# Dense products of a hybrid decoder layer: the 544 tokens split at 512 in place of 272

## The reference

```python
x = x + 0.5 * swiglu_1(rmsnorm(x))                 # 1024 -> 2816 (gate, up) -> 1024
z = rmsnorm(x) @ w_in                              # 1024 -> 3608: mLSTM and GLA heads
x = x + concat(mlstm(z), gla(z)) @ w_out           # 1024 -> 1024
x = x + cross_attention(rmsnorm(x), memory)        # w_q, 256 memory tokens, w_o
x = x + 0.5 * swiglu_2(rmsnorm(x))
y = final_rmsnorm(x)
```

## Time and profile before

| | us |
|---|---|
| median of 2 runs (1354.36 to 1355.21) | 1354.78 |
| the profiled execution, its own time | 1352.57 |
| its span, first to last instruction | 1350.7 |
| TensorE busy (98%) | 1327.1 |
| weight loads busy (95%) | 1289.6 |
| DVE busy (49%) | 665.2 |
| ACT busy (32%) | 429.3 |
| mean granted TensorE clock, share of full | 0.995 |

### The profile page before, as it was taken

How to read it: one execution, slowest core, us unless ns; L and a number is a source line. 1 busy time by engine, 2 the same in 40 slices (tenths; PEclk the granted TensorE clock), 3 DMA queues, 4 the chain that set the end, 5 groups by cost and what they waited for, 6 DMA issues and landing times.

```text
span 1350.7 us, 25765 instructions
## 1 busy us (share of the span) xinstructions
PE 1327.1 (98%) x11027; PEld 1289.6 (95%) x11027; DVE 665.2 (49%) x903; ACT 429.3 (32%) x644; POOL 41.8 (3%) x64
## 2 busy tenths in 40 slices
PE   8999999999999999999999999999999999999997
PEld 8999999999999999998888898889999999999997
DVE  5445455443333377667676534535545445443332
ACT  6222222222222243345434612323322222222222
POOL 1000000000000000002111000100000000000000
PEclk9999999999999999999999999999999999999998
DMA  6332323323333333224145664533232232323221
GB/s 198 95 92 79 93 82 88 89 73 88 91 79 95 81 79 80 79 79 126 35 124 191 220 208 141 212 101 94 79 93 86 85 93 81 90 85 88 86 71 67
DMA packets 208136, 138.31 MB, mean 102 GB/s; under 512 B 6550, under 2 KB 196224, under 8 KB 208068
## 3 DMA queue, kind: packets, MB, share of 16 engines
q1 hardware_dynamic: 200240, 109.88, 28.1%
q0 software_dynamic: 7664, 27.27, 6.1%
q10 hardware_dynamic: 164, 0.16, 0.0%
HBM read 129.41 MB, written 7.88 MB: 102 GB/s over the span
## 4 chain that ended last, share of the span: by engine, by line
PE 48%; DVE 1%; ACT 1%; issue 0%; another core or an unknown queue 0%; ACTq 0%
PE ps L1690 47%; PE ps L2135 1%; PE ps L2239 0%; ACT prob L873 0%; PE ps L2164 0%; DVE xmx L1563 0%; PE ps L2085 0%; DVE kT L1580 0%; PE ps L2113 0%; ACT kT L884 0%; DVE v_own L1457 0%; DVE y_raw L1401 0%; DVE prob L1572 0%; ACT y_hi L805 0%
## 5 line engine op out<-in xcount | busy, mean ns | idle before, releaser
L1690 PE MATMUL ps<-xn_hi,w_hi 128*128 128x272 f32 x2144 | 447.2, 289 | 0.9 <-ACT xn_hi L573 0.9
L1690 PE MATMUL ps<-xn_hi,w_lo 128*128 128x272 f32 x2144 | 444.1, 288 | 0.0
L1690 PE MATMUL ps<-xn_lo,w_hi 128*128 128x272 f32 x2144 | 442.7, 287 | 0.6 <-DVE xn_lo L985 0.6
L551 ACT ACTIVATE w_hi<-raw 128x1024 fp32r<-128x1024 f32 x206 | 218.0, 1058 | 642.5 <-PE ps L1690 642.5
L967 DVE TENSOR_TENSOR w_lo<-raw,w_hi 128x1024 fp32r<-128x1024 f32 x206 | 252.3, 1225 | 201.8 <-ACT w_hi L551 200.7
L1690 PEld LDWEIGHTS ps<-xn_hi,w_hi 128*128 128x128 f32 x2144 | 336.1, 188 | 2.1 <-DVE w_lo L967 1.1
L1690 PEld LDWEIGHTS ps<-xn_hi,w_lo 128*128 128x128 f32 x2144 | 337.7, 189 | 0.0
L1690 PEld LDWEIGHTS ps<-xn_lo,w_hi 128*128 128x128 f32 x2144 | 336.1, 188 | 1.0 <-DVE xn_lo L985 0.8
L1690 PE MATMUL ps<-h_hi,w_hi 128*128 128x272 f32 x704 | 145.9, 289 | 0.0
L1690 PE MATMUL ps<-h_hi,w_lo 128*128 128x272 f32 x704 | 145.3, 288 | 0.0
L1690 PE MATMUL ps<-h_lo,w_hi 128*128 128x272 f32 x704 | 144.9, 287 | 0.0
(11 more groups left out here) (345 smaller groups left out, 1087.4 us busy)
## 6 DMA issues: line engine op xcount, KB each, us to landing
raw<-in_ffn_w_gate SPq DMA_DIRECT2D x44, 512.0 KB, 3.9
raw<-in_ffn_w_up SPq DMA_DIRECT2D x44, 512.0 KB, 3.8
raw<-in_w_in SPq DMA_DIRECT2D x29, 512.0 KB, 3.8
raw<-in_ffn_w_down SPq DMA_DIRECT2D x32, 448.0 KB, 3.7
raw<-in_ffn_w_down SPq DMA_DIRECT2D x16, 512.0 KB, 3.9
kv<-in_cache_mem_k POOLq DMA_DIRECT2D x6, 1024.0 KB, 6.3
kv<-in_cache_mem_v POOLq DMA_DIRECT2D x6, 1024.0 KB, 6.9
raw<-in_w_out SPq DMA_DIRECT2D x8, 512.0 KB, 4.1
```

What stands on the lines that cost most here:

```text
L551: act.activation(w_hi[u0 % 2][:, :], raw[u0 % 4][:, :], ACT.Copy).then_inc(sem("hi_done"), 1)
L1690: return pe.matmul(out, lhsT, rhs, start=start, stop=stop)
```

## The change

A pair of halves becomes a long part of 512 tokens (the prompt, TP) and a short part of 32 (the sample). The long part fills the first bank of its pair, the short part columns 0 to 31 of the second, so that the 544 results lie in one run and `halves` becomes the identity. The waits by half follow the new parts: the first needs all four prompt chunks, the second the sample too. The small decay product, in its own banks, keeps 272 and 272.

```diff
@@ pair @@
-            return ps[:, q:q + 2, 0:HT]
+            return ps[:, q:q + 2, :].rearrange("p b c -> p (b c)")[:, 0:T]
+
+        SPLIT = [(0, TP), (TP, T)]
@@ halves @@
-            return t2d.rearrange("p (h t) -> p h t", h=2)
+            return t2d
@@ norm @@
-                mm(pair(buf)[:, 0, :], ones, acc[:, 0:HT])
-                mm(pair(buf)[:, 1, :], ones, acc[:, HT:T]).then_inc(sem("norm_mm"), 1)
+                mm(pair(buf)[:, 0:TP], ones, acc[:, 0:TP])
+                mm(pair(buf)[:, TP:T], ones, acc[:, TP:T]).then_inc(sem("norm_mm"), 1)
@@ unit @@
-                            ins = mm(ps[:, 2 * (buf % 4) + half, 0:HT], w, m[:, k0 + j, half * HT:(half + 1) * HT],
+                            t0, t1 = SPLIT[half]
+                            ins = mm(ps[:, 2 * (buf % 4) + half, 0:t1 - t0], w, m[:, k0 + j, t0:t1],
                                      first and j == 0 and n == 0, last and j == nk - 1 and n == 2)
@@ out_half @@
-                pe.wait_ge(sem("ym_lo"), NC - 1 if half == 0 else NC + 1)
+                pe.wait_ge(sem("ym_lo"), NC + half)
@@ first unit of the attention's output product @@
-                pe.wait_ge(sem("av_lo"), NC - 1 if half == 0 else NC + 1)
+                pe.wait_ge(sem("av_lo"), NC + half)
```

More of the change, by code:

```diff
@@ L1271, in _ @@
                     for n in range(2):
-                        ins = dve.tensor_scalar(halves(decay[:, n, :]), ps[:, 4 + 2 * n:6 + 2 * n, 0:HT],
+                        ins = dve.tensor_scalar(decay[:, n, :].rearrange("p (h t) -> p h t", h=2), ps[:, 4 + 2 * n:6 + 2 * n, 0:HT],
                                                 gains[:, G_BA + n:G_BA + n + 1], None, ALU.add)
```

## The result

The changed kernel takes 1869.37 us (1868.34 to 1870.39), 1.379 times the time before (95% interval 1.377 to 1.382). The forecast, 1750 us and slower, had the direction and most of the size, but the time lies above the range (1705 to 1820).

The account below looks back on a forecast made before the run. TensorE's dense products were taken as the bound, with 4464 pairs growing by exposed weight loads. 1352.6 + 396 (pairs) + 0.6 (norms) - 0.8 (a wait gone) = 1748, about 1750 us; range 1705 to 1820.

Parts of the forecast that it names:

- The bound: Whole kernel: TensorE's dense products, 4464 pairs, 1117 us of 1352.6; a change in pair length enters the time in full.
- The pair: Dense products: long matmul 228 ns plus short one 111 ns, 339 ns against 250.2; times 4464, 396 us more.
- spacings of 20 to 65 ns behind short matmuls: Sign of a wrong forecast: in the products, the next long matmul starts this soon after a short one.
- a clock of 0.50 in the products: Sign of a wrong forecast: TensorE's granted clock at half speed (1.2 GHz) during the dense products.
- the clock falls: Rival, dense products: thinner columns, 70% of the pair, lower TensorE's clock to 0.50; over 2300 us if throughout; chance 3%.
- The waits by halves: Output product and attention's output product: no new wait for prompt chunks; a wait of some 0.8 us for the sample goes.
- Loads run ahead: Rival, dense products: weights load two sets ahead under the long matmul; pair 250 ns, time stays 1353 us; chance 6%.
- a cheaper load: Rival, dense products: an exposed load costs 62 ns, pair 290 ns, +178 us, 1530 us; chance 5%.
- Norms: Four plain f32 sums over partitions: each 1.07 us for 0.91, four times +0.16, under 1 us.
- reading: DVE and ACT read 544 columns as one run over two banks: same number of elements, no change in time.

Follow-up runs that it names:

- e5: Changed kernel with only the 72 short matmuls that run apart (second halves of three units) repeating the sample's columns to 256; 1799.6 us.
- e10: Changed kernel, keeping its layout and waits, with the split set back to 272 and 272 columns; 1355.8 us, 1.0007 of the time before.
- e3: Changed kernel with long matmuls, but for the first and last of each accumulation, using only 64 of 128 weight columns; 1559.4 us, ratio 1.151.

## Why the prediction was right or wrong

**The bound** was right: every nanosecond of the pair went into the time, and no other engine came near. DVE's busy time is 666.0 us against 665.2, ACT's 430.1 against 429.3.

**The pair** was right in mechanism and 5 ns short: 344 in place of 339, with bounds of 331 and 354. The exposed load has its 108 to 111 ns. The long matmul is the term that was mis-sized: 344 - 111 = 233 ns, not 228, and by themselves long matmuls stand 232 apart; the memory product's rows had 229 on average. 5 ns times 4464 are 23 us, so the forecast at the full clock should have been 1772, well inside its range. One sign of being wrong was badly chosen: spacings of 20 to 65 ns behind short matmuls do stand in the records (0.03 us), and yet the load is exposed, since the wait lies inside the long one's record. The other sign, a clock of 0.50 in the products, came, and rightly.

**The rival "the clock falls" was wrong as it was put.** It was given 3% and one price, over 2300 us, for a clock that falls throughout. What happened is that mechanism in three places, for 214 us, at 99 us. This is what carried the time out of the range. Two steps failed. The first is the row held against it, the clock at 1.00 with matmuls of one column: it is 1.3 us long, and it was used for a stream of hundreds of microseconds. Nor need a fall come at once: the train from 1187.5 to 1190.1 itself ran at 1.00, and the low clock is in the stretch from 1191.4 on. The second is that the question was asked only of the pairs, not of the short halves by themselves: the part *The waits by halves* says that splitting a step into long and short halves doesn't change its sum. The sum at the full clock is the same; but 48 and 24 short matmuls in a row, with hardly any columns, are a stretch of their own. Before, these halves had 272 columns each. e5 shows that padding these 72 matmuls takes both dents away. The dent behind the decay product has no train in front of it, and that product is the same in both kernels. Behind it no fall came in the kernel before; in e10, which has the same 272 and 272, one came and was over after 3.4 us, where the changed kernel's lasted 51:

```profile
460.60:464.00 3.40, 3.40 (x25) 3.34 (x19) 0.00 (x0) 0.00 (x0) 0.00 (x0) 0.50 0.57 154
464.10:480.00 15.90, 15.90 (x129) 15.90 (x128) 7.69 (x12) 5.35 (x5) 0.00 (x0) 1.00 0.16 38
```

So a fall that costs next to nothing between equal halves is drawn out by the new pairs, and for that the sum had no term.

**Loads run ahead** and **a cheaper load** were refuted by the same rows that spoke against them: two loads of a tile 0.11 us apart, and no load under the long matmul but one; e3 shows that the load is what is paid. The Trainium skill's reorder window ("TensorE: Matmul & The Clock Gate", "Step-by-step: what each phase is for"), which the prediction names for the first of these, shows here only as one load ahead.

**Norms, reading, waits** were right in being small. The output product's first load is at 905.04 and the last prompt chunk's y_lo, started at 902.46 with 1.23 us, was done before it; the sample's ended at 912.48, and the first halves ran to 916.5, so nothing waited (DVE and loads of the kernel after):

```profile
902.46 1.23 DVE L1409 TENSOR_TENSOR y_lo<-y_raw,y_hi 128x1024 fp32r<-128x1024 f32 x1 [0.70 <-ACT y_hi L807]
...
912.05 0.43 DVE L1512 TENSOR_TENSOR y_lo<-ew,y_hi 128x256 fp32r<-128x256 f32 x1 [0.49 <-ACT y_hi L846]
```

```profile
905.04 0.19 PEld L1692 LDWEIGHTS ps<-y_hi,w_hi 128*128 128x128 f32 x1
```

e10, with these edits and 272 columns, is within 0.2% of the kernel before.

## What to carry to other kernels

Where each matmul brings its weights, price a stream as the sum, over its matmuls, of the longer of two: this matmul's columns and the load for the next; equal columns in fewer, longer matmuls are not equal time when the rest is shorter than a load. Then read the clock's row for each stretch that an edit makes sparser, the short ones by themselves too, and price a fall by how long the stream behind it stays low, not as all or nothing. Padding a matmul that hides nothing can be free, and here it was worth 105 us.

## What the runs showed of the hardware that was not expected

What the clock did in these runs depended on what it was: pairs of 512 and 32 columns ran at 1.00 for hundreds of microseconds, and the same pairs stayed at 0.50 for 123 us after 24 short matmuls, with TensorE busy throughout. With 128 columns in the short one the falls lasted 3.4 to 6.8 us in the products, and 3.4 us too behind e3's train of 24 with pairs of 0.29 us. A matmul's record can begin before its weights are loaded: 0.03 us behind the load's start, where the load takes 0.11. A weight load is twice as long at half the clock, 0.21 us in place of 0.11. And 288 columns before 256 are 2.8 ns a pair quicker than twice 272, which makes 1344.4 us, 0.8% under the kernel before (interval 0.7% to 1.0%), the quickest version of this study.
